# Mixer A's values a round later and four-row scores in all nine rounds: a two-layer hybrid decoder trunk on one core

## The reference

```python
proj = einsum('btd,dn->btn', x, w_in[l])              # 2578 columns
# A: 6 heads, two maps each (q1,k1 and q2,k2, 32 wide), causal
p = softmax(q1 k1) - lam * softmax(q2 k2)
o_a = p @ v; o_a = o_a * rsqrt(mean(o_a**2) + eps) * subln_g * (1 - lam_init)
# B: causal means over windows of 2, 4, 8, 16, minus the value, times w_pool and pool_scale
# C: 6 query heads, 2 key/value groups, 64 wide; three causal branches, mixed by sigmoid gates
#    compressed (31 blocks), selected (all 8 blocks of 64 are chosen), sliding window (all 512)
mix = concatenate([o_a, o_b, o_c]) @ w_out[l]
x = layer_norm(ALPHA * x + mix, ln1_g[l], ln1_b[l])
x = layer_norm(ALPHA * x + square(relu(x @ w_up[l])) @ w_down[l], ln2_g[l], ln2_b[l])
```

## Time and profile before

| | us |
|---|---|
| median of 3 runs | 1260.44 (1260.19 to 1260.78) |
| the profiled execution | 1260.26 |
| its span | 1258.4 |
| TensorE matmul busy | 1237.9 |
| VectorE, GpSimd, ScalarE busy | 725.6, 493.0, 477.6 |

### The profile page before, as it was taken

One profiled execution on the slowest core, in us unless ns is written; L12 is line 12 of the kernel. 1 busy time (PEld: TensorE's weight loads), 2 busy tenths in 40 slices (PEclk: granted clock), 3 DMA queues, 4 the chain that ended last, 5 costly groups with the idle time before them and its releaser, 6 DMA issues.

```text
span 1258.4 us, 17853 instructions
## 1 busy us (share of the span) xinstructions
PE 1237.9 (98%) x7118; PEld 1028.7 (82%) x7118; DVE 725.6 (58%) x1117; ACT 477.6 (38%) x946; POOL 493.0 (39%) x279
## 2 busy tenths in 40 slices
PE   7999999999999999999999999999999999999997
PEld 7998766789888888888899976668988888888885
DVE  4395778369672262360397868783796623605406
ACT  5226688523232221222143366784333322222210
POOL 3468000134544444444345760003264444444442
PEclk9999999999999999999999999999999999999999
DMA  7433001123523332233224320013233332332211
GB/s 252 124 80 102 2 18 35 67 84 102 162 94 101 101 99 88 98 101 96 63 60 128 93 68 1 18 52 100 69 129 105 101 100 89 97 101 101 96 55 67
DMA packets 77826, 110.04 MB, mean 87 GB/s; under 512 B 17648, under 2 KB 38448, under 8 KB 77616
## 3 DMA queue, kind: packets, MB, share of 16 engines
q1 hardware_dynamic: 76160, 104.11, 27.4%
q10 hardware_dynamic: 1584, 4.78, 1.2%
HBM read 106.78 MB, written 2.10 MB: 87 GB/s over the span
## 4 chain that ended last, share of the span: by engine, by line
PE 91%; DVE 4%; issue 1%; ACT 1%; POOL 1%; DMA 0%; DVEq 0%; POOLq 0%; ACTq 0%
PE ps L678 16%; PE ps L679 16%; PE ps L680 16%; PE ps L675 9%; PE ps L674 9%; PE ps L676 9%; PE ps L781 3%; PE ps L769 3%; PE ps L818 2%; PE ps L803 1%; PE ps L633 1%; DVE negmax L1390 1%; ACT probs_a L1134 1%; PE ps L894 1%; PE ps L856 1%
## 5 line engine op out<-in xcount | busy, mean ns | idle before, releaser
L542 POOL TENSOR_TENSOR w_lo<-raw,w_hi 128x1024 fp32r<-128x1024 f32 (+3 forms) x184 | 425.0, 2314 | 644.7 <-ACT w_hi L1006 644.2
L1006 ACT ACTIVATE w_hi<-raw 128x1024 fp32r<-128x1024 f32 (+3 forms) x200 | 199.0, 996 | 598.2 <-PE ps L680 365.7
L674 PE MATMUL ps<-xt_hi,w_lo 128*128 128x512 f32 (+1 forms) x576 | 210.7, 366 | 0.0
L675 PE MATMUL ps<-xt_hi,w_hi 128*128 128x512 f32 (+1 forms) x576 | 210.5, 365 | 0.0
L676 PE MATMUL ps<-xt_lo,w_hi 128*128 128x512 f32 (+1 forms) x576 | 210.5, 365 | 0.0
L678 PE MATMUL ps<-w_hi,xt_lo 128*128 128x384 f32 (+3 forms) x448 | 152.0, 339 | 1.6 <-DVE xt_lo L1242 1.1
L678 PE MATMUL ps<-w_hi,mt_lo 128*128 128x512 f32 x384 | 150.1, 391 | 0.0
L679 PE MATMUL ps<-w_hi,mt_hi 128*128 128x512 f32 x384 | 149.4, 389 | 0.0
L680 PE MATMUL ps<-w_lo,mt_hi 128*128 128x512 f32 x384 | 149.4, 389 | 0.0
L680 PE MATMUL ps<-w_lo,xt_hi 128*128 128x384 f32 (+3 forms) x448 | 147.5, 329 | 0.0
L679 PE MATMUL ps<-w_hi,xt_hi 128*128 128x384 f32 (+3 forms) x448 | 147.4, 329 | 0.0
(11 more groups left out here) (175 smaller groups left out, 1875.1 us busy)
## 6 DMA issues: line engine op xcount, KB each, us to landing
raw<-in_w_up SPq DMA_DIRECT2D x64, 512.0 KB, 3.7
raw<-in_w_down SPq DMA_DIRECT2D x64, 512.0 KB, 3.9
raw<-in_w_in SPq DMA_DIRECT2D x32, 384.0 KB, 3.3
raw<-in_w_in SPq DMA_DIRECT2D x16, 256.0 KB, 2.8
raw<-in_w_in SPq DMA_DIRECT2D x32, 128.0 KB, 2.9
raw<-in_w_out SPq DMA_DIRECT2D x8, 512.0 KB, 3.4
raw<-in_w_out SPq DMA_DIRECT2D x12, 256.0 KB, 3.7
rows<-in_ln_g ACTq DMA_DIRECT2D x4, 512.0 KB, 4.3
```

Of the source, the lines that this page charges most:

```text
L542: nc.gpsimd.tensor_tensor(unit_of(w_lo, u), unit_of(raw, u), unit_of(w_hi, u).bitcast(F32), ALU.subtract).then_inc(s_lo_ready, 1)
L674: mm(o, wl[:, c], a_hi[:, k, cols], start=first, stop=False)
L675: mm(o, wh[:, c], a_hi[:, k, cols], start=False, stop=False)
L1006: A(unit_of(w_hi, u), unit_of(raw, u), ACT.Copy).then_inc(s_hi_ready, 1)
```

## The change

In mixer A, `values` of a round moves behind the scores that follow the next one: at an odd t TensorE does scores of both maps for t + 1, values of t - 2, the chunk, the side steps and then the turn. All nine rounds of A use `scores_of_both`. In C, values of t - 1 comes ahead of the turn of t, except for the last two tasks; ScalarE's weight split for the output projection comes behind the copy. Two of the pooling mixer's steps and two of the compressed branch's change places. At the head, GpSimd's first two weight splits of layer 0 go to VectorE, between its splits of x. At the tail, tile 3 comes last, in two halves, each stored by itself.

```diff
-BOTH = 6
+BOTH = 9
@@ SIDE
-        10: (("square_sums", 0, 5),), 14: (("turn", 13, 5), ("turn", 14, 6)), 15: (("cmp_turn", 0, LAST_BANK),),
-        16: (("box", 0, 5), ("box", 1, 6)), 17: (("cmp_turn", 1, LAST_BANK),), 18: (("square_sums", 1, LAST_BANK),),
+        10: (("square_sums", 0, 5),), 14: (("turn", 13, 5), ("turn", 14, 6)), 15: (("box", 0, LAST_BANK),),
+        16: (("cmp_turn", 0, 5), ("cmp_turn", 1, 6)), 17: (("box", 1, LAST_BANK),), 18: (("square_sums", 1, LAST_BANK),),
@@ SP, after the last layer
-            for n, tt in enumerate((0, 1, 3, 2)):
-                sp.wait_ge(s_out_last, n + 1)
+            for tt in range(3):
+                sp.wait_ge(s_out_last, tt + 1)
                 sp.dma_start(out[0, tt * P:(tt + 1) * P, :], xres[:, tt]).then_inc(s_stored, 16)
-            sp.wait_ge(s_stored, 16 * TT)
+            for half in range(2):
+                sp.wait_ge(s_out_last, 4 + half)
+                c = slice(512 * half, 512 * half + 512)
+                sp.dma_start(out[0, 3 * P:4 * P, c], xres[:, 3, c]).then_inc(s_stored, 16)
+            sp.wait_ge(s_stored, 16 * (TT + 1))
@@ POOL
-                if layer == 0:
-                    split(layer, 0, 2)
@@ PE, side
+                if t < TASKS_A and t % 2 == 0:
+                    pe.wait_ge(s_p_copied, nth("p_copied", layer, turn_number(t - 1) + 1))
@@ PE, side_step, box (and gone from cmp_turn)
+                    pe.wait_ge(s_in_copied, nth("in_copied", layer, TT * IN_CHUNKS))
@@ PE, the loop over t
-                    for n in LAST_AT.get(t, ()):
-                        last_chunk(layer, n)
                     if 2 * BOTH - 2 <= t < TASKS - 2:
                         scores(layer, t + 2)
-                    if turns(t):
+                    if t < TASKS_A and t % 2:
+                        if t >= 3:
+                            values(layer, t - 2)
+                        for n in LAST_AT.get(t, ()):
+                            last_chunk(layer, n)
+                        if t in SIDE:
+                            side(layer, t)
                         turn_p(layer, t)
-                    if t >= 1 and turns(t - 1):
-                        values(layer, t - 1)
-                    if t in SIDE:
-                        side(layer, t)
+                    elif t < TASKS_A:
+                        for n in LAST_AT.get(t, ()):
+                            last_chunk(layer, n)
+                        if t in SIDE:
+                            side(layer, t)
+                    else:
+                        if t < TASKS - 2:
+                            values(layer, t - 1)
+                            turn_p(layer, t)
+                        else:
+                            turn_p(layer, t)
+                            values(layer, t - 1)
+                        if t in SIDE:
+                            side(layer, t)
@@ ACT, the loop over t: the two lines move from ahead of copy_p(t - 1) to behind it
-                    if t in OUT_SPLIT:
-                        split_to(layer, U_OUT + OUT_SPLIT.index(t) + 1)
@@ DVE, scale_and_shift and the last norm
-                def scale_and_shift(tt):
+                def scale_and_shift(tt, parts=1):
...
-                        if tt in (0, 1, 3):
+                        if tt < 2:
                             scale_and_shift(tt)
                     scale_and_shift(2)
+                    scale_and_shift(3, 2)
@@ DVE, head of layer 0
-                    split_x(layer, 0, 0, range(5))
+                    low_unit(layer, 0)
+                    split_x(layer, 0, 0, (0, 1))
+                    low_unit(layer, 1)
+                    split_x(layer, 0, 0, (2, 3, 4))
                     low_unit(layer, 2)
```

More of the change, by code:

```diff
@@ L875, in side_step @@
                     pe.wait_ge(s_cmp_probs, nth("cmp_probs", layer, 1))
-                    pe.wait_ge(s_in_copied, nth("in_copied", layer, TT * IN_CHUNKS))
                     for i in range(2):
@@ L1170, in _ @@
                         copy_p(t - 1)
+                    if t in OUT_SPLIT:
+                        split_to(layer, U_OUT + OUT_SPLIT.index(t) + 1)
                     if t in LAST_COPIED:
@@ L1247, in low_unit @@
                 g = layer * UNITS + u
-                dve.wait_ge(s_lo_ready, nth("lo_ready", layer, u))
+                if g:
+                    dve.wait_ge(s_lo_ready, nth("lo_ready", layer, u))
                 dve.wait_ge(s_hi_ready, nth("hi_ready", layer, u + 1))
@@ L1288, in sums_of @@
                     V.tensor_scalar(mv[:, tt, 1:2], mv[:, tt, 1:2], LN_EPS, None, ALU.add).then_inc(s_stats, 1)
-                def scale_and_shift(tt):
+                def scale_and_shift(tt, parts=1):
                     dve.wait_ge(s_rstd, nth("rstd", layer, TT + tt + 1))
                     dve.wait_ge(s_out_centred, tt + 1)
-                    V.scalar_tensor_tensor(xres[:, tt], xres[:, tt], rstd[:, tt:tt + 1], rows[:, 1], ALU.mult, ALU.add) \
-                        .then_inc(s_out_last, 1)
+                    n = D // parts
+                    for c in range(0, D, n):
+                        xs = xres[:, tt, c:c + n]
+                        V.scalar_tensor_tensor(xs, xs, rstd[:, tt:tt + 1], rows[:, 1, c:c + n], ALU.mult, ALU.add).then_inc(s_out_last, 1)
                 if final:
```

## The result

The changed kernel takes 1266.27 us (median of 5 runs, 1264.94 to 1267.99), the kernel before 1260.47 (1260.19 to 1260.78): ratio 1.0049, 95% interval 1.0038 to 1.0059. It is 0.5% slower; the forecast was 1265.6. The profiled execution took 1264.94, so 1.3 less than the median.

The account below looks back on a forecast made before the run. TensorE, busy 1237.9 of 1258.4 us, was taken as the bound, with ScalarE and VectorE over 80% busy where C runs. 1260.26 + 7.2 (3.6 per layer) - 1.4 (head) - 0.5 (tail) = 1265.6 us; 8-in-10 range 1259.8 to 1268.8.

Parts of the forecast that it names:

- Four-row scores save 3.0 us: Mixer A, rounds 6 to 8: scoring both maps together takes 3.0 us of TensorE work less per layer.
- Waits of A: 5.75 new, 1.45 gone: Mixer A, per layer: new TensorE waits at scores and side steps sum to 5.75 us; about 1.45 us of old ones go.
- Side steps at the same total: Mixer A: box and compressed-turn steps swap places at no cost; box's new wait for the input copies is already met.
- +1.3: Mixer A's net per layer: -3.0 + 5.75 - 1.45, so side 18 ends 1.3 us later than before.
- The price is a loop that two-map scores close: Mixer A: scores of both maps wait for the previous round's exponentials; loop 6.0 us, 5.2 in 384 rounds, showing after t = 13.
- C's order, 0.8 + 0.7 + 0.85 = 2.35: Mixer C, us per layer: 0.8 at values for squares (t = 18), 0.35 each at scores 30 and 31, 0.85 at the end.
- just fits: Mixer C, weight split at t = 25: no wait, because the next exponentials are the short ones (1.35 us).
- Head -1.4, tail -0.5: Head: two weight splits moved to VectorE gain 1.4 us; tail: earlier first store and tile 3 in halves gain 0.5.
- 1: Rival: the loop doesn't bind and no more new waits come than the 2.25 that go; 1252.4 us, chance 0.08.
- 2: Rival: C's order and end are free, only A's +1.3 per layer stays; 1261.0 us, no change, chance 0.18.
- 3: Rival: ScalarE's squares and copies also delay the next round's maxima, 5.5 us per layer; 1269.4 us, chance 0.10.
- Rival 4: New gaps halve TensorE's clock for 20 us behind t = 12 in both layers, adding 30 us or so; 1290, chance 0.01.

Follow-up runs that it names:

- two-bank run: The changed kernel with four-row scores for six rounds of mixer A instead of nine (BOTH = 6), against the kernel before: 1271.68 us, ratio 1.0090.

## Why the prediction was right, and where it was not

The time (1265.6 against 1266.27) and the places of all the larger waits were right. Several terms were not, and that the sum came so near is in part luck: errors of both signs met.

- **Four-row scores save 3.0 us.** 2.5 in the old order: TensorE's busy time in A falls from 68.33 to 65.83 with four rows alone. In the new order it is 2.95. What the steps stand beside makes the difference; it was not taken apart.
- **Waits of A: 5.75 new, 1.45 gone.** Idle time rose by 3.4 us net, not 4.3. The whole window had 1.12 of idle time before, so 1.45 could not go. The waits stood where I put them, scores 10, side 10, scores 12, side 14, scores 16, at 0.65, 0.85, 0.82, 0.90, 0.64 for 0.85, 1.05, 0.95, 1.05, 0.75: each 0.1 to 0.2 smaller. The small ones (0.25 to 0.3 at scores 6, 18, 19) were not seen; side 6 showed 0.17.
- **Side steps at the same total.** Wrong by 0.41 where they were exchanged alone, in the old order. In the changed kernel some 0.4 of busy time is left over (a saving of 2.5 by the four rows, 2.1 measured), from the order and the exchange together. So A's +1.32 for +1.3 is luck: 0.5 less saved, 0.9 less waited, 0.4 that I had at nothing.
- **"The price is a loop that two-map scores close."** Right in the old order, where four rows save 2.5 and cost 3.6. In the order of the changed kernel it is not what sets the waits: without the four rows 3.73 of its 4.54 us of idle time are still there, and with them A is 2.1 us shorter. My sum of a gain by the four rows and a loss by the waits gives the right total for both together and the wrong share for each: the four rows and the place of the values act on each other.
- **C's order, 0.8 + 0.7 + 0.85 = 2.35.** The waits came to 1.09, 0.90 (0.17 + 0.55 + 0.18) and 1.03 (0.74 more at turn 31, 0.29 at turn 32), together 3.0, and the split at t = 25, which "just fits", costs 0.17. Left out was a gain of 0.9 in busy time: the round of t = 26 takes 211.14 - 207.80 = 3.34 for 3.44, since a turn in front of masks takes 0.93 and one in front of values 1.02. Net 2.13.
- **Head -1.4, tail -0.5.** In the profiled execution 1.6 and 0.5. But that is the best head of thirteen profiles, which gain 0.9 on average, and over many runs both together are worth 1.2 for the 1.9 in the sum. That the head's share varies by over a microsecond I had not seen.
- **Rivals.** 1, 2 and 3 are out: A's and C's waits both came, and near my size. Rival 4, which I gave 0.01, is real in its mechanism and was wrong in price: not 20 us at half clock in every layer but some 3.4 us in some layers (an estimate from the three windows, (0.22 + 0.50 + 0.13) x 2 / 0.50), 1.5 to 1.6 us each time. Whether it is why the median lies 1.3 us above the profiled execution is not shown: the execution at the median has a mean granted clock of 0.998, like the profiled one, and the profiled one had the best head. Over the ten executions of the changed kernel, the four with 0.998 took 1264.94 to 1266.27, the six with 0.996 or 0.997 1266.25 to 1267.99. The Trainium skill, TensorE: Matmul & The Clock Gate, section HAM oscillation, tells of idle gaps that lower the clock, with waits longer than these; the granted 0.50 in 166 to 168 agrees that waits of TensorE can do it. My sentence that the trace shows none of that for waits so short held for the kernel before alone, and "1.00 in all stretches" left out its last one, 0.82 in 1240 to 1259, where the work runs out.

## What to carry to other kernels

When TensorE is 98% busy, removing its work pays only as far as the other engines' round is shorter than what remains; follow one round of each engine before pricing the saving. A step that is queued first in a round needs its input a round early: put what can run at once ahead of what waits (values ahead of scores gained 0.6 us per layer here), and put extra work of the second engine (here weight splits) into the rounds in which it idles, which was worth 1.1 us per layer. Where two edits act on the same waits, run all four combinations; one corner alone misled me twice.

## What the runs showed of the hardware that I had not expected

- Behind waits of 0.90 and 0.65 us (ended at 162.92 and 164.66) the granted clock fell to 1.2 GHz in one profile of the changed kernel; the other profile has the same waits to 0.01 us and granted 1.00. In the two-bank run it fell behind a wait of 1.29 in layer 1, and stayed at 1.00 behind the same wait in layer 0.
- The same TensorE step takes 0.09 to 0.1 us more or less by what follows: a turn of eight tiles 1.02 in front of values and 0.93 in front of masks; exchanging four small side steps cost 0.41 us per layer without a wait.
- TensorE's first products of 384 columns took 0.52 us each in some heads and 0.33 in others, at a granted clock of 1.00 in the windows of both (head and tail alone, changed kernel). Their starts are 0.32 us apart for 0.17; in the two-bank run, at a granted 0.50, products of 512 columns are 0.43 apart for 0.23, the same ratio. So it looks like the lower clock, which the granted clock does not show here; that is argued, not shown.
- VectorE's cast took 1.28 us beside GpSimd's split and 0.29 without, and a subtraction 1.94 and 0.43; each slow one ended 0.14 and 0.29 us after the split beside it.
